# The last token tile of a hybrid decoder layer in halves, its routing with fewer dependent steps, one weight unit asked for sooner

## Chip, core and metric

One Trainium2 chip, one of its cores. The metric is the device time of one execution in microseconds, of the runs' median. The profile shows one more execution, taken by the hardware profiler.

## The reference, cut to what matters

One decoder layer over 512 prompt tokens and 8 sampled tokens (520 rows of 1024, float32). A mixer (a state-space part and a gated chunk part, joined by one output projection `w_out` and a residual add) is followed by a mixture of experts:

```
x = x + mix @ w_out
t = rmsnorm(x, norm2_g)
gl = t @ w_router_group + b;  gi = argmax(gl)              # 4 groups
el = (t @ w_router_expert + b)[group gi]                   # 8 experts in it
top 2 of softmax(el), weights normalised, times softmax(gl)[gi]
x = x + sum over the two experts e:  weight_e * (silu(t @ w_gate[e]) * (t @ w_up[e])) @ w_down[e]
y = rmsnorm(x, final_norm_g)
```

There are 32 experts with 1024x512, 1024x512 and 512x1024 weights each, 201 MB in all, every one of them read once.

## The kernel before

**Stages.** Everything is written out by hand in one program per engine, joined by semaphores. The first part (to about 190 us) is the mixer. Then come the five token tiles, in the order `ORDER = (0, 4, 1, 2, 3)`: 128 rows each, tile 4 the 8 sampled rows. `n` is the place in that order, `t` the tile, so `n = 4` is tile 3, the last. Each goes through the same steps:

- TensorE: output projection `out_half(t, j, halves)`, `j` the half of the mixer it takes, `halves` the 512-column halves of the result in `own[t]` (two PSUM banks). Tile 3's is spread between the other tiles' steps, and its last pieces are `out_half(3, 0, (0,))` and `out_half(3, 0, (1,))`. The semaphore `o_ps` counts finished tiles.
- VectorE: residual add into `x2` (loop at L1004, recorded as L694, the line of the helper `tt`; `o_ev`).
- ScalarE: `square` (L572, L574), `x2T_copy` (L587), `normed` (L579, with the store of the normalised rows to `hn2_d`, L581). VectorE: `root` (L955).
- TensorE: `turn` (eight transposes, L1363), `logits` (L1358, 36 columns).
- VectorE: `top_two` (L963 to L986): the best group, the two best experts as one-hot rows `oh12`, and their sum `ohb`. Of several equal values the first is taken, by a running count (`first_of`). The second expert's hits are found with the first one's taken out, so the two follow each other.
- TensorE: `count_before`, how many rows before this one go to the same expert. VectorE: `place` (L988 to L1002) makes of it the row's place `Wp` in the expert's list, the quotient `Wq` by 64 and remainder `Wr`; `row_oh` is the one-hot of the remainder over 64 places, `Wm` the mask of those with quotient 0, and `entry` the token number (two small parts, `vals`) of the masked rows at their expert's column.

**Table.** After the last tile ten small products (`row_oh` by `entry`, five tiles by two experts) give the table of 64 token numbers for each expert. `rows_of` (L1033) turns them into row numbers, an empty place into a large one (v = 0 gives 4000, out of bounds, so that the gather leaves it out). GpSimd then gathers the rows of experts 0 and 1 from `hn2_d` (`fetch_first`), and TensorE turns them (`x_T`). What does not fit an expert's 64 places goes through a second table (`xentry`, `further_table`) and loops of further steps.

**Experts.** 32 steps, each `gate_up`, a turn and `down` with 64 rows. The weights come as 96 units of 2 MB into a ring of ten places (`NSLOT = 10`), all issued by SyncE in order; `load(q)` is unit `q`:

```
            sp.wait_ge(wo_used, 1)
            load(6)
            store_x2(NT - 1)
            sp.wait_ge(o_ps, NT)
            sp.wait_ge(lg_ps, NT)
            load(7)
            sp.wait_ge(hn2_out[0], 48)
            sp.wait_ge(hn2_out[1], 32)
            load(8)
            sp.wait_ge(x2_out, 16 * NT)
            sp.wait_ge(xg_in[0], 16)
            load(9)
```

Places 6 to 9 hold other data in the first part, so these loads wait for it to be used: place 7 the half of `w_out` that the last `out_half` reads. Unit 10 and all behind it wait for the expert step that frees their place (`gu_half` halfway through `gate_up`, `gu_ps` at its end, `dn_ps` after `down`).

**Busy products.** `keep_busy(n)` is n products of the identity with itself, of two instructions each, whose result is not used. They fill TensorE's waits: 6 before the last count, 5 before the table, 12 and 8 between the table and the turn of the gathered rows.

Of the kernel before, what the change touches and what calls it, by code (L numbers as in the profile page):

```python
# [7 lines left out]
D = 1024  # L8
# [3 lines left out]
NT = 5  # L12
# [18 lines left out]
INVALID = 4000  # L31
# [9 lines left out]
def build(nc, a, o):  # L41
# [3 lines left out]
    with ctx:  # L45
# [107 lines left out]
        halfpi = tiny[:, 72:73]  # L153
        g2 = tiny[:, 84:92]
# [5 lines left out]
        def small(at, *shape):  # L160
            return view(23808 + at, *shape)
# [21 lines left out]
        sv = small(266, 2, 2)  # L183
# [143 lines left out]
        def _(sp):  # L327
# [96 lines left out]
        def _(act):  # L424
# [151 lines left out]
            def normed(n, t):  # L576
                r = ROWS[t]
                act.wait_ge(rt_rdy, n + 1)
# [104 lines left out]
        def _(dve):  # L683
# [255 lines left out]
            V.memset(Wq, 0.0)  # L939
            V.memset(Wm, 0.0)  # L940
# [22 lines left out]
            def top_two(n, t):  # L963
                r = ROWS[t]
                dve.wait_ge(lg_ps, n + 1)
                dve.wait_ge(rt_rdy, n + 1)
# [10 lines left out]
                mine, hit, count = (s32[0:r, k, :] for k in range(3))  # L977
# [4 lines left out]
                link(V.tensor_scalar(hit, mine, m8[0:r, t, 0:1], None, ALU.is_equal))  # L982
                link(first_of(oh1, hit, count))
                link(V.scalar_tensor_tensor(hit, mine, m8[0:r, t, 1:2], oh1, ALU.is_equal, ALU.is_gt))
                link(first_of(oh2, hit, count))
                tt(ohb[0:r, t, :], oh1, oh2, ALU.add).then_inc(oh_rdy, 1)  # L986

            def place(n, t):  # L988
# [5 lines left out]
                link(tt(s32[0:r, 3, 0:16].rearrange("p (j k) -> p j k", j=2), Wp[0:r, t, :].unsqueeze(2).to_broadcast([r, 2, 8]),  # L994
                        thr[0:r].unsqueeze(1).to_broadcast([r, 2, 8]), ALU.is_ge))
                link(V.tensor_reduce(Wq[0:r, t, :], s32[0:r, 3, 0:16].rearrange("p (j k) -> p j k", j=2), AX.X, ALU.add))
                V.scalar_tensor_tensor(Wr[0:r, t, :], Wq[0:r, t, :], float(-C), Wp[0:r, t, :], ALU.mult, ALU.add)
                link(V.tensor_scalar(Wm[0:r, t, :], Wq[0:r, t, :], 0.5, None, ALU.is_lt))
                tt(row_oh[0:r, t], rank_at[0:r].unsqueeze(1).to_broadcast([r, 2, C]), Wr[0:r, t, :].unsqueeze(2).to_broadcast([r, 2, C]), ALU.is_equal)
                link(tt(sv[0:r], vals[0:r, t], Wm[0:r, t, :].unsqueeze(2).to_broadcast([r, 2, 2]), ALU.mult))  # L1000
                tt(entry[0:r, t], oh12[0:r, t].unsqueeze(3).to_broadcast([r, 2, NE, 2]),
                   sv[0:r].unsqueeze(2).to_broadcast([r, 2, NE, 2]), ALU.mult).then_inc(slot_rdy, 1)  # L1002

            for n, t in enumerate(ORDER):  # L1004
# [12 lines left out]
                if n == 4:  # L1017
                    place(3, 2)
# [4 lines left out]
                if n == 3:  # L1023
# [4 lines left out]
                    place(2, 1)  # L1028
            top_two(4, 3)
# [3 lines left out]
            def rows_of(out, ps, n):  # L1033

                hi, lo = (ps[0:C, 0:2 * n].rearrange("c (t w) -> c t w", w=2)[:, :, w] for w in range(2))
                v, none, row, less = (ids[:, k, 0:n] for k in range(4))
                link(V.tensor_scalar(none, hi, 8.0, None, ALU.mult))
                link(tt(v, none, lo, ALU.add))
                link(V.tensor_scalar(none, v, 0.0, float(INVALID + 1), ALU.is_equal, ALU.mult))
                link(V.scalar_tensor_tensor(row, v, -1.0, none, ALU.add, ALU.add))  # L1040
                link(V.tensor_scalar(less, row, float(NTOK), float(-NTOK), ALU.is_ge, ALU.mult))
                tt(out[:, :, 0], less, row, ALU.add)
# [772 lines left out]
```

## Time and profile before

| | us |
|---|---|
| median of 3 runs | 762.81 (762.32 to 763.8) |
| profiled execution, as timed | 764.95 |
| its span in the profile | 763.2 |
| busy: TensorE products | 661.4 (87%) |
| busy: VectorE | 276.0 (36%) |
| busy: ScalarE | 160.6 (21%) |
| busy: GpSimd | 89.2 (12%) |
| weights and activations moved | 246.53 MB, mean 323 GB/s |

How to read it: times inside the profile count from the span's start. A line number is that of the kernel before. Many operations of VectorE go through one helper and carry its line, L694; all products carry L1358, all turns L1363, so they are told apart by their tiles and shapes. A float32 product appears as two MATMUL instructions. The DMA share is the mean busy share of the core's 16 DMA engines.

### The profile page before, as it was taken

The numbers are of one execution on the slowest core, as the hardware profiler recorded it, in microseconds if no ns is written. First come the engines' busy times: TensorE is split into PE (matmuls) and PEld (weight loads), VectorE is DVE, ScalarE is ACT, GpSimd is POOL, SyncE is SP. The second block draws the span as 40 slices with busy tenths as digits, with TensorE's granted clock in tenths as the row PEclk, the third lists the DMA queues.
The fourth block names the chain that finished last, engine by engine and source line by source line (L and its number), as shares of the span: only waits on it lengthen the run. The fifth ranks groups of instructions, "written<-read, shape, count | busy, mean of one in ns | idle before, by whom it ended". The sixth has DMA issues, their size and how long they took to land.

```text
span 763.2 us, 9485 instructions
## 1 busy us (share of the span) xinstructions
PE 661.4 (87%) x3284; PEld 322.6 (42%) x3284; DVE 276.0 (36%) x564; ACT 160.6 (21%) x314; POOL 89.2 (12%) x161
## 2 busy tenths in 40 slices
PE   8999989999997899996799997778777776769794
PEld 4488878854547433332233332223222222223231
DVE  7798994394475311210011121111111111112047
ACT  3687410321413011110111110101001110001023
POOL 4100000000001112121011211111111111111000
PEclk9999999999996899997899999999999999999998
DMA  9432017378247899999999999999999999999982
GB/s 331 191 110 112 1 40 280 135 314 381 88 165 284 307 406 403 396 390 388 427 416 398 411 408 394 418 406 410 413 395 401 405 413 406 402 398 415 421 329 112
DMA packets 29573, 246.53 MB, mean 323 GB/s; under 512 B 6578, under 2 KB 7090, under 8 KB 16592
## 3 DMA queue, kind: packets, MB, share of 16 engines
q1 hardware_dynamic: 22784, 233.95, 76.2%
q0 software_dynamic: 5280, 8.20, 3.3%
q10 hardware_dynamic: 1456, 3.62, 1.3%
q8 instruction: 41, 0.67, 0.4%
q14 instruction: 12, 0.10, 0.0%
HBM read 235.65 MB, written 19.20 MB: 334 GB/s over the span
## 4 chain that ended last, share of the span: by engine, by line
PE 51%; DMA 27%; DVE 13%; ACT 3%; another core or an unknown queue 3%; issue 2%; SPq 1%; ACTq 0%; POOLq 0%; DVEq 0%
PE psA L1358 27%; PE psB L1358 23%; DMA mem<-in_w_gu 19%; DMA mem<-in_w_down 5%; DVE mem L694 5%; DMA mem<-y_d 1%; DVE mem L918 1%; DVE mem L1173 1%; DMA mem<-in_w_vb 1%; DMA y_d<-mem 1%; ACT front_c L627 1%; PE psA L1363 1%; DVE mem L833 1%; PE psB L1363 1%
## 5 line engine op out<-in xcount | busy, mean ns | idle before, releaser
L1358 PE MATMUL psA<-mem 128*64 128x512 f32 (+8 forms) x1380 | 316.9, 521 | 39.9 <-DMA mem<-in_w_gu 20.6
L1358 PE MATMUL psB<-mem 128*64 128x512 f32 (+6 forms) x1242 | 276.0, 542 | 37.3 <-DMA mem<-in_w_gu 16.4
L1358 PEld LDWEIGHTS psA<-mem 128*64 128x64 f32 (+4 forms) x1380 | 148.4, 155 | 189.7 <-issue 139.2
L1358 PEld LDWEIGHTS psB<-mem 128*64 128x64 f32 (+2 forms) x1242 | 114.8, 155 | 180.0 <-issue 138.9
L694 DVE TENSOR_TENSOR mem<-mem 128x512 f32<-128x512 f32 (+21 forms) x124 | 68.1, 565 | 24.0 <-ACT mem L541 19.6
L1278 POOL DMA_INDIRECT y_d<-front_c,mem x30 | 27.5, 916 | 288.6 <-DVE front_c L1083 288.6
L1111 DVE TENSOR_TENSOR front_c<-front_c,psA 64x512 f32<-64x512 f32 x15 | 10.4, 690 | 122.5 <-ACT front_c L627 122.5
L1111 DVE TENSOR_TENSOR front_c<-front_c,psB 64x512 f32<-64x512 f32 x15 | 10.3, 690 | 122.1 <-ACT front_c L627 122.1
L1273 POOL DMA_INDIRECT mem<-hn_d,mem x34 | 33.3, 979 | 98.1 <-DVE mem L1043 70.5
L627 ACT ACTIVATE front_c<-psA 64x512 f32<-64x512 f32 x15 | 8.8, 588 | 125.8 <-PE psA L1358 125.8
L627 ACT ACTIVATE front_c<-psB 64x512 f32<-64x512 f32 x15 | 8.8, 588 | 116.5 <-PE psB L1358 116.5
L1083 DVE COPY front_c<-psA 64x512 f32<-64x512 f32 x15 | 10.4, 693 | 55.6 <-PE psA L1358 55.6
L1083 DVE COPY front_c<-psB 64x512 f32<-64x512 f32 x15 | 10.4, 693 | 52.6 <-PE psB L1358 52.6
L1363 PE MATMUL psA<-ident,mem 64*128 64x64 f32 (+2 forms) x200 | 19.1, 239 | 5.8 <-DMA mem<-hn_d,mem 4.5
L638 ACT ACTIVATE front_c<-psA 64x512 f32<-64x512 f32 x15 | 8.9, 591 | 71.0 <-PE psA L1358 71.0
L638 ACT ACTIVATE front_c<-psB 64x512 f32<-64x512 f32 x15 | 8.9, 590 | 69.9 <-PE psB L1358 69.9
L1363 PEld LDWEIGHTS psA<-ident,mem 64*128 64x128 f32 (+2 forms) x200 | 16.4, 142 | 9.7 <-issue 6.9
L1358 PE MATMUL psB<-ident 128*128 128x128 f32 x80 | 15.5, 376 | 3.4 <-POOL mem L1224 2.0
L694 DVE TENSOR_TENSOR mem<-psA,tiny 128x512 f32<-128x512 f32 x18 | 12.4, 691 | 10.4 <-PE psA L1363 8.6
L1363 PE MATMUL psB<-ident,mem 64*128 64x64 f32 (+1 forms) x152 | 13.5, 228 | 3.0 <-DVE mem L1098 3.0
L694 DVE TENSOR_TENSOR mem<-psB,mem 128x512 f32<-128x512 f32 (+2 forms) x23 | 15.0, 705 | 3.1 <-PE psB L1358 3.1
L1358 PEld LDWEIGHTS psB<-ident 128*128 128x128 f32 x80 | 14.6, 283 | 3.6 <-POOL mem L1224 2.0
(233 smaller groups left out, 373.7 us busy)
## 6 DMA issues: line engine op xcount, KB each, us to landing
mem<-in_w_gu SPq DMA_DIRECT2D x64, 2048.0 KB, 40.1
mem<-in_w_down SPq DMA_DIRECT2D x32, 2048.0 KB, 42.2
mem<-in_w_out SPq DMA_DIRECT2D x2, 2048.0 KB, 8.7
y_d<-mem SPq DMA_DIRECT2D x1, 4096.0 KB, 11.8
mem<-y_d SPq DMA_DIRECT2D x8, 512.0 KB, 9.1
mem<-in_x_T SPq DMA_DIRECT2D x8, 260.0 KB, 8.7
mem<-in_w_vb SPq DMA_DIRECT2D x8, 256.0 KB, 8.9
mem<-in_x_prompt SPq DMA_DIRECT2D x4, 512.0 KB, 11.1
```

The lines of the kernel that those rows point to most:

```text
L627: A(sg[64:128, u, :], ps[0:64, 1, :], ACT.Silu).then_inc(sg_rdy, 1)
L638: A(yst[0:C, u, 0:512], ps[0:64, 3, :], ACT.Copy).then_inc(y0_ev, 1)
L694: return V.tensor_tensor(out, x, y, op)
L833: V.tensor_copy(*u_copy(ql, e, 1))
L918: V.tensor_copy(mixA[32 * ql:32 * ql + 32, :, 0:NP_].rearrange("p m (b i) -> p i m b", i=T)[:, i], yg[32 * i:32 * i + 32, ql, :, NS:YC])
L1083: V.tensor_copy(yst[0:C, u, 512:1024], (psA, psB)[u][64:128, 3, :]).then_inc(y1_ev, 1)
L1111: V.tensor_tensor(hh[0:64, u, :], sg[64:128, u, :], ps[64:128, 1, :], ALU.mult).then_inc(h_done, 1)
L1173: ins = V.scalar_tensor_tensor(x2[0:r, t, :], yin[0:r, 2 * t + j, :], cw[0:r, j, t:t + 1], x2[0:r, t, :], ALU.mult, ALU.add)
L1273: return G.indirect_dma_start(out=dst, out_offset=None, in_=hn2_d[:, :], in_offset=bass.IndirectOffsetOnAxis(ap=rows_ap, axis=0), bounds_c ...
L1278: return G.indirect_dma_start(out=y2_d[:, :], out_offset=bass.IndirectOffsetOnAxis(ap=rows_ap, axis=0), in_=src, in_offset=None, bounds_ch ...
L1358: return nc.tensor.matmul(out, lhsT, rhs, start=start, stop=stop, skip_group_check=True)
L1363: return nc.tensor.transpose(out, in_, ident[b0:b0 + p, b0:b0 + p])
```

## The change

- Tile 3 is added (`add_half`), turned (`turn_half`), copied and multiplied with the router (`logits_half`) in two halves of 512 columns. `o_ps` now counts the two halves of its projection apart, the first at the end of `out_half(3, 0, (0,))`; the second to last places (`place(3, 2)`) stand between the two adds. The square is taken in halves too; the first half's mean enters the root as its bias.
- `top_two` finds both experts' hits from the values alone and counts both; where the two values are equal the second takes the second hit (`second` is 2 then, else 1). `entry` is made there, of the unmasked numbers.
- `place` compares the ranks with the place itself, without quotient, remainder or mask: a place of 64 or more matches none. Quotient, remainder and mask are made for all tiles together behind the first table, and `row_oh` once more with the remainder.
- The table products of the first four tiles go ahead of the last tile's count; two remain behind it. The busy products become 6, 2, 8 and 5 (from 6, 5, 12 and 8).
- `rows_of` needs no step for empty places: the token numbers are stored less 2048 (`EMPTY`), which is added back, so an empty place is 2048. The signal to GpSimd moves from the second output to the first; the second follows without one.
- SyncE issues unit 7 ahead of the last `x2` store and waits for the last projection only.

```diff
@@ SyncE
-                sp.wait_ge(o_ev, n + 1)
+                sp.wait_ge(o_ev, n + 1 if n < NT - 1 else NT + 1)
...
             load(6)
+            sp.wait_ge(o_ps, NT + 1)
+            load(7)
             store_x2(NT - 1)
-            sp.wait_ge(o_ps, NT)
             sp.wait_ge(lg_ps, NT)
-            load(7)
@@ ScalarE
-            for n in range(1, NT):
+            for n in range(1, NT - 1):
...
+            act.wait_ge(hn2_out[0], 32)
+            act.wait_ge(o_ev, NT)
+            A(hn2[:, 0, 0:512], x2[:, 3, 0:512], ACT.Square, accum_out=half_ss).then_inc(n2sq, 1)
+            for h in range(2):
+                act.wait_ge(x2T_ps, NT + h)
+                A(hn2T[:, 4 * h:4 * h + 4, :], own[3][:, h, :].rearrange("p (b n) -> p b n", n=128), ACT.Copy).then_inc(x2T_ev, 1)
+            act.wait_ge(o_ev, NT + 1)
+            A(hn2[:, 0, 512:1024], x2[:, 3, 512:1024], ACT.Square, accum_out=ss[:, 0, 3:4]).then_inc(n2sq, 1)
+            act.wait_ge(n2sq, NT + 1)
+            act.wait_ge(rt_rdy, NT)
+            A(ss[:, 1, 3:4], ss[:, 0, 3:4], ACT.Sqrt, scale=1.0 / D, bias=half_mean).then_inc(n2rt, 1)
+            normed(NT - 1, 3)
@@ VectorE, top_two
-                link(V.tensor_scalar(hit, mine, m8[0:r, t, 0:1], None, ALU.is_equal))
-                link(first_of(oh1, hit, count))
-                link(V.scalar_tensor_tensor(hit, mine, m8[0:r, t, 1:2], oh1, ALU.is_equal, ALU.is_gt))
-                link(first_of(oh2, hit, count))
+                V.tensor_scalar(hit1, mine, m1, None, ALU.is_equal)
+                V.tensor_scalar(hit2, mine, m2, None, ALU.is_equal)
+                link(V.tensor_scalar(second[0:r], m1, m2, 1.0, ALU.is_equal, ALU.add))
+                V.tensor_tensor_scan(count1, one32[0:r], hit1, 0.0, ALU.mult, ALU.add)
+                link(V.tensor_tensor_scan(count2, one32[0:r], hit2, 0.0, ALU.mult, ALU.add))
+                V.scalar_tensor_tensor(oh1, count1, 1.0, hit1, ALU.is_equal, ALU.mult)
+                link(V.scalar_tensor_tensor(oh2, count2, second[0:r], hit2, ALU.is_equal, ALU.mult))
                 tt(ohb[0:r, t, :], oh1, oh2, ALU.add).then_inc(oh_rdy, 1)
+                tt(entry[0:r, t], oh12[0:r, t].unsqueeze(3).to_broadcast([r, 2, NE, 2]),
+                   vals[0:r, t].unsqueeze(2).to_broadcast([r, 2, NE, 2]), ALU.mult)
@@ VectorE, last tile
+            dve.wait_ge(x_in[1], X_ROWS[1] * 16)
+            add_half(0)
+            place(3, 2)
+            dve.wait_ge(n2sq, NT)
+            V.tensor_scalar(half_mean, half_ss, 1.0 / D, EPS, ALU.mult, ALU.add).then_inc(rt_rdy, 1)
+            add_half(1)
+            root(4, 3)
             top_two(4, 3)
             place(4, 3)
@@ TensorE
-            out_half(3, 0, (0,))
+            out_half(3, 0, (0,)).then_inc(o_ps, 1)
...
             out_half(3, 0, (1,)).then_inc(o_ps, 1)
-            turn(4, 3)
-            logits(4, 3)
+            turn_half(0)
+            turn_half(1)
+            logits_half(0)
+            logits_half(1)
+            pe.wait_ge(slot_rdy, 4)
+            for n, t in enumerate(ORDER[0:4]):
+                table_rows(t, n == 0, False)
             keep_busy(6)
```

TensorE from the last output half (the first row) to the turn of the gathered rows (the last; `ident,mem 128x64`). Before:

```order
L1358 MATMUL psA<-mem 128x512 x4
L1363 MATMUL psA<-ident,mem 128x128 x8
L1358 MATMUL psA<-mem 128x36 x8
L1358 MATMUL psB<-ident 128x128 x6
L1358 MATMUL psA<-ohb,oneb 128x32 x4
L1358 MATMUL psA<-ohb,trib 128x32
L1358 MATMUL psB<-ohb,oneb 128x32 x5
L1358 MATMUL psB<-ident 128x128 x5
L1358 MATMUL psA<-mem 64x64 x10
L1358 MATMUL psB<-ident 128x128 x12
```

Changed:

```order
L1386 MATMUL psA<-mem 128x512 x4
L1391 MATMUL psA<-ident,mem 128x128 x8
L1386 MATMUL psA<-mem 128x36 x8
L1386 MATMUL psA<-mem 64x64 x8
L1386 MATMUL psB<-ident 128x128 x6
L1386 MATMUL psA<-ohb,oneb 128x32 x4
L1386 MATMUL psA<-ohb,trib 128x32
L1386 MATMUL psB<-ohb,oneb 128x32 x5
L1386 MATMUL psB<-ident 128x128 x2
L1386 MATMUL psA<-mem 64x64 x2
L1386 MATMUL psB<-ident 128x128 x8
```

Eight of the ten table products (64x64) have moved up behind the logits, ahead of the six busy products; seven busy products less stand on the way, counting those before the turn of the gathered rows (5, not 8; that turn and the register loads between stand behind the rows shown).

VectorE from the mask sum of the last tile (`ohb`) to the row numbers. Before:

```order
L694 TENSOR_TENSOR ohb<-mem 128x32
L694 TENSOR_TENSOR mem<-mem,psA 128x64
L993 TENSOR_REDUCE mem<-mem 128x2
L694 TENSOR_TENSOR mem<-mem 128x16
L996 TENSOR_REDUCE mem<-mem 128x2
L997 SCALAR_TENSOR_TENSOR mem<-mem 128x2
L998 TENSOR_SCALAR mem<-mem 128x2
L694 TENSOR_TENSOR mem<-mem 128x128
L694 TENSOR_TENSOR mem<-mem 128x4
L694 TENSOR_TENSOR mem<-mem 128x128
L1037 TENSOR_SCALAR mem<-psA 64x32
```

Changed:

```order
L707 TENSOR_TENSOR ohb<-mem 128x32
L707 TENSOR_TENSOR mem<-mem 128x128
L707 TENSOR_TENSOR mem<-mem,psA 128x64
L1011 TENSOR_REDUCE mem<-mem 128x2
L707 TENSOR_TENSOR mem<-mem 128x128
L1060 TENSOR_SCALAR mem<-psA 64x32
```

The entry (the first 128x128) now stands ahead of the row that waits for the count (`mem,psA`); behind that row two are left of eight.

SyncE's DMAs around the last x2 store:

```order
@@ -41,6 +41,6 @@
 L365 DMA x_d<-mem 128x1024 x2
 L329 DMA mem<-in_w_gu 128x4096
+L329 DMA mem<-in_w_down 128x4096
 L365 DMA x_d<-mem 128x1024
-L329 DMA mem<-in_w_down 128x4096
 L329 DMA mem<-in_w_gu 128x4096 x2
 L329 DMA mem<-in_w_down 128x4096
```

Unit 7 (`in_w_down`) is issued ahead of the last x2 store.

## Rows read from the trace of the kernel before

**Rows 1.** The page's second part: DMA's busy tenths in 40 slices of the span

```profile
DMA  9432017378247899999999999999999999999982
```

**Rows 2.** Stretches; busy us (count) of PE, PEld, DVE, ACT, POOL, clock, DMA share, GB/s

```profile
300.00:310.00 10.00, 9.80 (x54) 3.62 (x52) 1.38 (x2) 0.97 (x2) 2.26 (x4) 1.00 1.00 402
```

**Rows 3.** SyncE's timeline: start us, us, DMA issued, how many

```profile
229.36 0.32 SPq L365 DMA_DIRECT2D x_d<-mem  x1
235.58 0.33 SPq L329 DMA_DIRECT2D mem<-in_w_down  x1
236.32 13.24 SPq L329 DMA_DIRECT2D mem<-in_w_gu  x2
256.40 0.33 SPq L329 DMA_DIRECT2D mem<-in_w_down  x1
```

**Rows 4.** Stretches of 4 us around the first expert, columns as before

```profile
232.00:236.00 4.00, 4.00 (x19) 4.00 (x20) 0.41 (x2) 2.13 (x2) 0.00 (x0) 0.50 0.35 135
...
248.00:252.00 4.00, 4.00 (x41) 3.69 (x40) 0.47 (x1) 0.00 (x0) 0.00 (x0) 0.92 0.53 135
256.00:260.00 4.00, 4.00 (x22) 1.29 (x19) 0.62 (x4) 0.16 (x1) 0.52 (x1) 1.00 0.75 205
```

**Rows 5.** The chain that ended last, 225 to 262 us: start us, us, what

```profile
224.54 3.54 PE psA L1358 x8
228.10 1.24 DVE mem L694
...
229.42 1.16 ACT mem L572 x2
...
231.86 3.64 PE psA L1358 x16
...
235.53 0.27 DVE mem L968
...
238.86 0.21 DVE ohb L694
...
239.70 0.23 DVE mem L694
...
241.64 0.82 PE psA L1358 x10
242.49 0.20 DVE mem L1037
...
243.13 0.20 DVE mem L1040
...
243.88 6.97 PE psB L1358 x40
250.86 0.65 PE psA L1363 x8
...
252.70 7.11 PE psA L1358 x32
```

**Rows 6.** Groups by line and form: count, busy us, mean ns

```profile
L694 DVE TENSOR_TENSOR mem<-psB,tiny 128x512 f32<-128x512 f32 x1 | 0.7, 690 | 0.0
...
L562 ACT ACTIVATE front_c<-mem 128x520 f32<-128x520 f32 x4 | 2.5, 638 | 10.1 <-DVE mem L694 10.1
```

**Rows 7.** TensorE's timeline, three pieces: start us, us, what, count

```profile
218.59 1.87 PE L1358 MATMUL psB<-mem 128*128 128x36 f32 x16
...
229.39 1.09 PE L1363 MATMUL psA<-ident,mem 128*128 128x128 f32 x8 [1.32 <-DVE mem L694]
...
235.30 2.91 PE L1358 MATMUL psB<-ident 128*128 128x128 f32 x12
```

**Rows 8.** Us from issue to landing: gathers (L1273), weight units (L329); hn_d stores' median

```profile
DMA to landing us min/median/max: 3.1/8.8/9.2
...
DMA to landing us min/median/max: 7.7/8.6/11.1
...
hn_d<-mem ACTq DMA_DIRECT2D x4, 512.0 KB, 3.0
```

More of the change, by code:

```diff
@@ L30 @@
 EPS = 1e-6
-INVALID = 4000
+EMPTY = 2048
 TWO_PI = 2.0 * math.pi
@@ L153, in build @@
         halfpi = tiny[:, 72:73]
+        half_ss, half_mean, second = (tiny[:, 74 + k:75 + k] for k in range(3))
         g2 = tiny[:, 84:92]
@@ L976, in top_two @@
                 link(V.tensor_scalar(s4[0:r, 2, :], s4[0:r, 2, :], -1.0, BIG, ALU.add, ALU.mult))
-                mine, hit, count = (s32[0:r, k, :] for k in range(3))
+                mine, hit1, count1, hit2, count2 = (s32[0:r, k, :] for k in range(5))
                 link(tt(mine.rearrange("p (g e) -> p g e", g=NG), el.rearrange("p (g e) -> p g e", g=NG),
@@ L993, in place @@
                 link(V.tensor_reduce(Wp[0:r, t, :], pr[0:r], AX.X, ALU.add))
[L994 to L1004, printed above, removed]
+                tt(row_oh[0:r, t], rank_at[0:r].unsqueeze(1).to_broadcast([r, 2, C]),
+                   Wp[0:r, t, :].unsqueeze(2).to_broadcast([r, 2, C]), ALU.is_equal).then_inc(slot_rdy, 1)
+            for n, t in enumerate(ORDER[0:4]):
                 if t < 4:
@@ L1028, in _, with add_half @@
                     place(2, 1)
+            def add_half(h):
+                dve.wait_ge(o_ps, NT + h)
+                half = x2[:, 3, 512 * h:512 * h + 512]
+                tt(half, own[3][:, h, :], half, ALU.add).then_inc(o_ev, 1)
+            dve.wait_ge(x_in[1], X_ROWS[1] * 16)
[5 more added lines that the diff above has]
+            root(4, 3)
             top_two(4, 3)
@@ L1035, in rows_of @@
                 hi, lo = (ps[0:C, 0:2 * n].rearrange("c (t w) -> c t w", w=2)[:, :, w] for w in range(2))
[L1036 to L1040, printed above, removed]
+                high, row, less = (ids[:, k, 0:n] for k in range(3))
+                link(V.tensor_scalar(high, hi, 8.0, float(EMPTY), ALU.mult, ALU.add))
+                link(tt(row, high, lo, ALU.add))
                 link(V.tensor_scalar(less, row, float(NTOK), float(-NTOK), ALU.is_ge, ALU.mult))
-                tt(out[:, :, 0], less, row, ALU.add)
+                tt(out[:, :, 0], less, row, ALU.add).then_inc(tbl_rdy, 1)
                 return V.tensor_copy(out[:, :, 1], row)
             dve.wait_ge(tbl_ps, 1)
-            rows_of(tbl, psA[:, 3, :], NE).then_inc(tbl_rdy, 1)
+            rows_of(tbl, psA[:, 3, :], NE)
             R = lambda j: rs[:, j, :]
@@ L1513, in turn, with turn_half, logits_half, table_rows @@
                 ins.then_inc(x2T_ps, 1)
+            def turn_half(h):
+                pe.wait_ge(o_ev, NT + h)
+                for k in range(4):
+                    ins = tr(own[3][:, h, 128 * k:128 * k + 128], x2[:, 3, 512 * h + 128 * k:512 * h + 128 * k + 128])
+                ins.then_inc(x2T_ps, 1)
+            def logits_half(h):
+                pe.wait_ge(x2T_ev, NT + h)
+                for k in range(4 * h, 4 * h + 4):
+                    ins = mm(own[3][:, 0, 64 * 4:64 * 4 + 36], hn2T[:, k, :], wr[:, k, :], k == 0, k == KD - 1)
+                if h:
+                    ins.then_inc(lg_ps, 1)
+            def table_rows(t, first, last):
+                r = ROWS[t]
+                for j in range(2):
+                    ins = mm(psA[0:C, 3, 0:2 * NE], row_oh[0:r, t, j, :], entry[0:r, t, j].rearrange("p e w -> p (e w)"),
+                             first and j == 0, last and j == 1)
+                if last:
+                    ins.then_inc(tbl_ps, 1)
             def logits(n, t):
@@ L1577, in _ @@
             ins.then_inc(tot_ps, 1)
-            keep_busy(5)
+            keep_busy(2)
             pe.wait_ge(slot_rdy, NT)
-            for n, (t, j) in enumerate(itertools.product(range(NT), range(2))):
-                r = ROWS[t]
-                ins = mm(psA[0:C, 3, 0:2 * NE], row_oh[0:r, t, j, :], entry[0:r, t, j].rearrange("p e w -> p (e w)"), n == 0, n == 2 * NT - 1)
-            ins.then_inc(tbl_ps, 1)
+            table_rows(3, False, True)
             pe.wait_ge(tbl_rdy, 1)
```

26 lines of the change are left out of this document (15 added, 11 removed).

## The prediction

> **What bounds the kernel now.** Read first the DMA line of the 40 slices [rows 1]: from the slice that begins at 267 us to the last but one, every digit is 9 or nearly so, while the slices before it are half empty. The stretches say it more sharply: at 300 us the 16 DMA engines are busy for the whole of their time at 402 GB/s [rows 2], but 0.53 of 248 to 252 us and 0.75 of 256 to 260 us [rows 4]. So there are two programs. Up to about 257 us a chain of small dependent steps sets the pace, and behind it the weight stream does.
>
> Who starts the stream? SyncE's own timeline [rows 3] shows weight unit 7 (the w_down row) at 235.58, unit 8 at 236.32, and unit 9 as the second of that pair, 13.24 us further down, so at 249.2: it waits for the first gather of rows. Unit 10 goes out at 256.40, halfway through the first expert. The ring has ten places, so all 86 units from 10 to 95 wait for an expert to be done with an old one. 86 units of 2048 KB are 180 MB; at 402 GB/s that is 449 us, from 257 to 706, and the queue never runs dry in between. Each microsecond that unit 10 goes out sooner is a microsecond off the end; a DMA made faster or sooner before it is worth nothing.
>
> So the question is how soon the first expert begins, and the chain of waits answers it [rows 5]: the last output half ends at 228.08, the residual add takes 1.24 us, then come square, copy and turn, the logits from 231.86, the choice of experts from 235.53 to 238.86, the places from 239.70, the table product at 241.64, the row numbers from 242.49, **6.97 us of products that only keep TensorE busy** from 243.88, the turn of the gathered rows (it begins with that piece's end, about 250.8), the first expert at 252.70.
>
> **The change, step by step** (all against the profiled execution: span 763.2 us, 764.95 us as timed).
>
> *Last tile in halves.* Before, nothing of tile 3 starts until 228.08, then 7.45 us pass to 235.53. After, the first half (added on VectorE while the second output half still runs, since the first output half is complete before 224.54) is only to be turned. From 228.08: add of the second half 0.69 [rows 6] to 228.8, meanwhile the first four turns; the other four (eight took 1.09 [rows 7]) to 229.35; on ScalarE the copy of half two, 0.6 by the 0.64 of a 520-column piece [rows 6], to 229.95. Then two branches. ScalarE: square of a half and the reading of its sum, 0.8 (whole they took 1.16 [rows 5], and a 520-column piece alone is 0.64 [rows 6]), then root and reciprocal of one column, some 0.5: 231.3. TensorE: the logits' first half runs beside that copy, so the 1.87 us of a whole logits product [rows 7] end near 231.2. The choice starts at 231.3, not 235.53: **4.2 us**. The bound below: before, the granted clock was 0.50 (the lower level, 1.2 GHz) in 232 to 236 us [rows 4] and this product took 3.64 us [rows 5], after three microseconds in which TensorE had only the turns to do. If it is at that level in the new order too, the logits end near 233.0, so 2.5 us. The new order leaves TensorE hardly a gap from 224.5 to 231, so I take 4.2.
>
> *Both experts side by side.* From the first hit to the mask sum there were seven dependent steps of some 0.25; now the two hits, the two counts and the two results follow each other without a wait between, and one small comparison is added. Such a step begins 0.21 after the one it depends on (three between 242.49 and 243.13 [rows 5]); one that depends on nothing begins sooner, I assume half of that. I count **0.3 us** (0.1 to 0.5). The entry product moves ahead of the place, behind the mask sum, where VectorE waits for TensorE anyhow (238.86 plus 0.2 to 239.70).
>
> *Places without a mask.* From 239.70 to 241.64, 1.94 us, nine instructions. Now three: product, sum and the wide comparison, twice 0.25 and 0.3, some 0.8. **1.1 us** (0.9 to 1.3). The quotient and remainder come later, for all tiles at once, behind the row numbers: five instructions, the last with 640 columns of output (512 took 0.69 [rows 6]), some 1.7 us, before the second table. That is only asked for behind the turn of the gathered rows, and VectorE has the whole wait for the gather, 243.88 to 250.8, for it: hidden, and if the cover should be short, at most a microsecond.
>
> *Table products.* Ten took 0.85, from 241.64 to 242.49; eight go ahead of the six busy products, where TensorE waits for the choice; two remain, 0.35. **0.5 us.** Their cover: logits end 231.3, eight products 0.7, twelve busy instructions 1.5 (full clock) to 2.9 (as at 235.30 [rows 7]), so TensorE is free between 233.5 and 234.9, and is asked for the mask sum at 234.5. It may be 0.3 late; I take that off.
>
> *Row numbers.* Two dependent steps of 0.21 [rows 5] go, and the signal moves ahead of the last copy (0.1): **0.5 us**.
>
> Sum to the first row table: 4.2 + 0.3 + 1.1 + 0.5 + 0.5 - 0.3 = 6.3, so 243.84 becomes 237.5.
>
> *Behind the table.* Twenty busy products (40 instructions) took 6.97 us and were longer than the gather, which was home at 249.2 (unit 9 went out on it [rows 3]), 5.4 us behind the table. Thirteen remain: 4.5 us at the same mix, 6.3 if each takes the 0.24 us of the twelve at 235.30 [rows 7]. The gather can now be the longer one: 5.4 if as before. It may be more, since unit 8 is then still in flight: gathers of 240 to 300 us land 3.1 to 9.2 us after their issue, median 8.8 [rows 8], and 3.1 was this one, since its issue took 1.0 and began 0.9 behind the table. I take 6.2 us for the later of the two: **0.7 us** (from +1.5 to -3.7).
>
> *Eighth unit sooner.* It goes out at about 228.3 instead of 235.58, into an idle DMA, but unit 9 and unit 10 wait for experts and not for it. Worth nothing by itself. It passes the last x2 store on SyncE's queue; that store is only asked for by unit 9. What it may cost is the normalised rows' store, issued at 232.6 instead of 232.9 and 3.0 us long when alone [rows 8]. It is home near 236, when the table is not (237.5), if it is not stretched by more than 1.5 us. Here the Trainium skill speaks against the change (DMA: Bandwidth & Descriptors, section Queues, rings and completion order): an engine takes turns between queue rows packet by packet, and a completion write goes out only after every earlier write of that engine, whatever its queue. By that the gather would be home no sooner than unit 8, and this part would be worth about nothing instead of 0.7. The trace agrees in kind: gathers beside the full queue take 8.8 us, not 3.1 [rows 8]. As a mechanism of its own it is rival B.
>
> Sum: 6.3 + 0.7 = **7.0 us** until the first expert, 245.7 instead of 252.70; unit 10 near 249.4. Against the profiled execution that is 764.95 - 7.0 = 757.95; the median of the runs shown, 762.81, stands 2.1 below it, and the prediction is given against the median: 762.81 - 7.0 = **755.8 us**.
>
> **The rivals.**
> *A, the clock in the first expert.* If the busy products run at full clock they end before the gather, TensorE idles some three microseconds, and the first expert begins at half clock, as the logits ran at 232. Half clock over 5 us of it loses 2.5. For it: busy products cut from 20 to 13, a longer wait; after the gaps at 228 to 232 the clock read 0.50 [rows 4]. Against: the busy products of before began at half clock (40 in 6.97, against 0.24 each at half), and 248 to 252 us reads 0.92 [rows 4]: full when the expert came. 7.0 - 2.5 = 4.5, so 758.3.
> *B, the gather behind unit 8.* Landing takes 8.8 and not 3.1: the turn comes 10.9 us after the table, 3.9 later than before, so 6.3 - 3.9 = 2.4 is left: 760.4.
> *C, slower: store and gather both behind weight units.* The store of the normalised rows, issued at 232.6, takes the 9.2 us of the slowest gather and not 3.0 [rows 8], home at 241.8; SP and GpSimd wait for it (unit 8 and the gather). Then 0.9 to the gather, 1.0 to issue, 8.8 to land: 252.5, against 250.8 before. Loss 1.7, so 764.5. It decides where the two landings together pass 16.3 us (they were 6.1). Against: unit 7 has over 4 us of head start, and units issued here are home after 7.7 at the least [rows 8], 5.2 of them at 402 GB/s, so little of it is left when the store is issued.
> *D, no effect:* the stream is not what ends last, or the shifted start meets another floor: 762.8. Against it speaks that no stretch behind 257 us has idle DMA.
> *E, more:* the gather as quick as before and the clock full: 6.6 + 1.5 = 8.1, so 754.7.
>
> **How the numbers follow.** Forecast 0.52; A 0.22; B 0.10; C 0.03; D 0.03; E 0.10. The range takes the forecast, A and E with their unknowns, and B's near part: 753.8 to 760.2. A measurement of this kernel tells 0.2%, 1.5 us, from nothing. Faster by more than that: all but C, D and a slice of B, 0.92; same 0.05; slower 0.03.
>
> **What would show it.** In the chain of waits of after: choice of experts for the last tile some 3 us behind the last output half and not 7.45; three instructions between the last places' wait and the table; the table 6.3 us sooner; the first expert at about 245.7. In the DMA timeline unit 7 at 228, unit 8 unmoved, units 9 and 10 sooner by what the first expert is. From there to the end the same distances as before. Wrong it would be if the first expert starts 7 us sooner and the end does not follow, or if SyncE's unit 8 goes out later than 237.

## The result and the profile after

| | before | changed |
|---|---|---|
| median of 8 runs each | 763.56 (762.32 to 764.78) | 766.31 (765.04 to 767.32) |
| ratio | | 1.0027, 95% interval 1.0014 to 1.0040 |
| span of the profiled execution | 763.2 | 765.6 |

The changed kernel is slower, by 0.27% or about 2.1 us by the ratio; the two medians lie 2.75 us apart. The forecast was 7 us the other way, and the result lies outside the range.

The chain of waits of the changed kernel from the last output half to the second expert (start us, us, what) tells it in nine rows:

```profile
228.47 0.70 DVE mem L707
...
230.40 0.72 ACT mem L610 x2
...
231.67 1.16 ACT mem L579
...
232.84 8.31 DMA hn_d<-mem
...
242.10 8.32 DMA mem<-hn_d,mem
...
250.47 1.11 PE psA L1391 x8
...
252.79 9.65 PE psA L1386 x32
...
262.47 0.60 ACT front_c L640
...
265.01 8.67 PE psB L1386 x32
```

Against [rows 5]: the add, the half square and the copy of the normalised rows end at 232.82. Then two DMAs stand in the chain where products and VectorE steps stood, 8.31 us for the store of the last normalised rows, and 8.32 us for the first gather. The turn of the gathered rows begins at 250.47 and not at 250.86, the first expert at 252.79 against 252.70. And that expert takes 9.65 us, not 7.11.

Where was the routing? VectorE's timeline (start, us, line, operation, names and shapes) shows it done long before. The rows are the logits' scaling, the mask sum, the first step of the last tile's places and the first of the row numbers:

```profile
231.75 0.26 DVE L980 SCALAR_TENSOR_TENSOR mem<-psA,tiny,mem 128x36 f32<-128x36 f32 x1
...
234.86 0.19 DVE L707 TENSOR_TENSOR ohb<-mem 128x32 bf16<-128x32 f32 x1
...
235.63 0.22 DVE L707 TENSOR_TENSOR mem<-mem,psA 128x64 f32<-128x64 f32 x1 [0.37 <-PE psA L1386]
...
236.77 0.18 DVE L1060 TENSOR_SCALAR mem<-psA 64x32 f32<-64x32 f32 x1 [0.34 <-PE psA L1386]
...
237.52 0.17 DVE L1064 CAST mem<-mem 64x32 int32<-64x32 f32 x1
```

Choice at 231.75, mask sum at 234.86, places from 235.63, row numbers from 236.77, table ready at 237.6. Before it was ready at 243.84 [rows 5]. But GpSimd issues the gather only when the store is home as well, and that was 3.5 us later, at 241.15. What was worked out for these engines came, and nothing of it reached the first expert.

SyncE's timeline answers to [rows 3]:

```profile
228.46 0.33 SPq L329 DMA_DIRECT2D mem<-in_w_down  x1
229.19 0.33 SPq L365 DMA_DIRECT2D x_d<-mem  x1
241.22 9.60 SPq L329 DMA_DIRECT2D mem<-in_w_gu  x2
259.03 0.33 SPq L329 DMA_DIRECT2D mem<-in_w_down  x1
```

Unit 7 goes out 7.1 us sooner; unit 8, which waits for the same store as the gather, goes out at 241.22 instead of 236.32; unit 10 at 259.03 instead of 256.40. The stretches answer to [rows 4] and [rows 2] (columns as there); the first row is the kernel before, the others are the changed one:

```profile
228.00:300.00 72.00, 63.64 (x361) 33.62 (x362) 25.19 (x96) 11.66 (x19) 9.12 (x15) 0.88 0.87 340
...
228.00:300.00 72.00, 58.69 (x329) 28.10 (x329) 22.41 (x83) 10.92 (x19) 9.10 (x15) 0.88 0.86 327
232.00:236.00 4.00, 2.65 (x28) 2.31 (x29) 3.21 (x19) 2.10 (x2) 0.00 (x0) 1.00 1.03 322
248.00:252.00 4.00, 1.53 (x16) 1.41 (x16) 0.38 (x1) 0.00 (x0) 0.00 (x0) 0.50 0.34 79
256.00:260.00 4.00, 4.00 (x16) 1.17 (x14) 0.50 (x4) 0.00 (x0) 0.37 (x1) 0.76 0.49 180
```

The clock is at full level in 232 to 236 us, where it was at half before, and at half in 248 to 252, just ahead of the first expert, where it was 0.92. The DMA share is 0.34 and 0.49 in the last two stretches (0.53 and 0.75 before). Over 228 to 300 us the DMAs moved 327 GB/s, before 340. That is 13 GB/s over 72 us, 0.94 MB, or 2.3 us at 402 GB/s, and the span grew by 2.4.

### The profile page after: what moved, and what is told of

Same layout as the page of the kernel before. It is cut to its first block, busy times and chain, and to the rows that moved or that the text cites. A ratio compares the mean times of both kernels' runs of the same rounds, so it can differ in the third digit from the quotient of the medians.

```text
span 765.6 us, 9429 instructions
## 1 busy us (share of the span) xinstructions
PE 659.7 (86%) x3264; PEld 317.9 (42%) x3264; DVE 272.9 (36%) x546; ACT 161.1 (21%) x317; POOL 89.2 (12%) x161
## 4 chain that ended last, share of the span: by engine, by line
PE 55%; DMA 28%; DVE 10%; ACT 3%; another core or an unknown queue 2%; issue 2%; SPq 0%; POOLq 0%; DVEq 0%
PE psA L1386 28%; PE psB L1386 25%; DMA mem<-in_w_gu 13%; DMA mem<-in_w_down 11%; DVE mem L707 4%; DVE mem L931 1%; DMA mem<-in_w_vb 1%; DMA mem<-hn_d,mem 1%; DMA hn_d<-mem 1%; ACT front_c L640 1%; PE psB L1391 1%; PE psA L1391 1%; DVE mem L846 1%; ACT mem L648 1%
## 5 line engine op out<-in xcount | busy, mean ns | idle before, releaser
L707 DVE TENSOR_TENSOR mem<-mem 128x512 f32<-128x512 f32 (+17 forms) x116 | 67.7, 598 | 23.7 <-ACT mem L541 19.6
L1391 PEld LDWEIGHTS psB<-ident,mem 64*128 64x128 f32 (+1 forms) x152 | 11.7, 139 | 6.6 <-issue 6.6
L1386 PE MATMUL psB<-ident 128*128 128x128 f32 x60 | 10.9, 355 | 2.9 <-POOL mem L1252 2.0
```

What stands on the lines that cost most here:

```text
L707: return V.tensor_tensor(out, x, y, op)
L1386: return nc.tensor.matmul(out, lhsT, rhs, start=start, stop=stop, skip_group_check=True)
L1391: return nc.tensor.transpose(out, in_, ident[b0:b0 + p, b0:b0 + p])
```

## The experiments

Twelve kernels in three groups, each timed beside the kernel before. A DMA is called home when it has landed, so when the engines that wait for it may go on. Half clock is a granted clock of 0.50, the lower level. Two suspects stood first: transfers that stand behind weight units, and the clock in the first expert. A third question came out of the first group: what the end of the kernel really follows.

### Unit 7 behind the store

```diff
-            sp.wait_ge(o_ps, NT + 1)
-            load(7)
             store_x2(NT - 1)
+            sp.wait_ge(o_ps, NT + 1)
             sp.wait_ge(lg_ps, NT)
             sp.wait_ge(hn2_out[0], 48)
             sp.wait_ge(hn2_out[1], 32)
+            load(7)
             load(8)
```

(Against the changed kernel, as every edit below unless it says otherwise.)

> The changed kernel with one difference: weight unit 7 is issued only once the last store of the normalised rows is home, together with unit 8. Theory (the store stands behind unit 7): the store takes 3 to 3.5 us instead of 8.3, the first gather is issued at about 238.5 instead of 242.1, but now has two units (10 us of transfer) ahead of it and lands near 249; first expert near 251.3, time 1.5 to 3 us below the changed kernel, near before (763 to 765). Rival (the clock in the first expert alone made the loss): the time stays at the changed kernel's. Rival (gathers are quick beside one or two units): gather home by 244, time near 758.

Ratio to before 1.0004 (0.9987 to 1.0022), median 763.81. The store's landing line, and the gather and the first expert in the chain of waits:

```profile
DMA to landing us min/median/max: 2.6/2.7/3.1
```

```profile
238.56 9.47 DMA mem<-hn_d,mem
...
248.07 1.11 PE psA L1391 x8
...
250.39 9.04 PE psA L1386 x32
```

The store takes 2.6 to 3.1 us. The gather goes out at 238.56, takes 9.47 with two units ahead of it, and the first expert begins at 250.39, at half clock (9.04 us long). Near what was expected; the loss is gone, nothing is won.

### The last x2 store behind the store

```diff
             load(7)
-            store_x2(NT - 1)
             sp.wait_ge(lg_ps, NT)
             sp.wait_ge(hn2_out[0], 48)
             sp.wait_ge(hn2_out[1], 32)
+            store_x2(NT - 1)
             load(8)
```

> The changed kernel with the last x2 store moved behind the store of the normalised rows on SyncE's side; unit 7 stays sooner. If the store of the normalised rows stands behind all that is queued ahead of it: home 1.3 us sooner (about 239.8), everything behind follows, time about 1 us below the changed kernel. If it was the x2 store alone that held it up: home near 236.5, the gather issued at 238.5, time 3 to 5 us below. If neither: 8.3 us and no difference.

Ratio 1.0023 (1.0007 to 1.0039), median 765.34. The slowest store is now 5.7 us, issued at 232.36 and home at 238.0: 2.6 us shorter, twice what was expected, so the x2 store had held it up too. But the gather, with unit 8 and the x2 store just ahead, took 9.72 instead of 8.32 and gave 1.4 us of it back; the first expert began at 251.06, again at half clock (8.65 us).

### Busy products until the gather is home

```diff
-            keep_busy(5)
+            keep_busy(38)
             pe.wait_ge(xg_in[0], 16)
```

> The changed kernel with 38 instead of 5 busy products ahead of the turn of the gathered rows, so that TensorE has work almost until the gather is home (250.4). Theory (half the clock in the first expert costs 2.5 us, and every microsecond of the first expert's end is one of the whole): the first expert takes 7.1 us instead of 9.65, time 2 to 3 us below the changed kernel, equal to before within 1 us. Rival (the weight stream, with its idle time before unit 10, sets the end by itself): first expert quick, but the time as the changed kernel's.

Ratio 0.9994 (0.9976 to 1.0011), median 763.45. The chain of waits:

```profile
237.39 13.49 PE psB L1386 x92
250.88 0.65 PE psA L1391 x8
...
252.60 7.11 PE psA L1386 x32
```

TensorE is busy for 13.49 us, the first expert begins at 252.60, as in the changed kernel, and takes 7.11 us. With that alone the loss is gone. Store and gather are nearly as slow as without this edit (7.5 us, and 8.4 from the start of the gather's issue to unit 9, which goes out on it); they have eaten the gain, and the clock made the loss.

### Only the sooner unit, in the kernel before

This edit is made to the kernel before:

```diff
-            store_x2(NT - 1)
             sp.wait_ge(o_ps, NT)
-            sp.wait_ge(lg_ps, NT)
             load(7)
+            store_x2(NT - 1)
+            sp.wait_ge(lg_ps, NT)
```

> The kernel before with only the eighth unit sooner. Theory: the store of the normalised rows takes 8 us instead of 3.3 (home near 241), unit 8 follows it 5 us later than before, and the first gather, issued as before at 244.7, has as much of the unit ahead of it as before had of units 7 and 8; so the time is that of before, within 1.5 us, and nothing is won by the sooner unit. Rival (a weight unit sooner is 5 us of transfer won): 2 to 5 us faster than before.

Ratio 1.0030 (1.0012 to 1.0048), median 766.3: slower, where I had expected no difference. The store took 8.1 us and unit 8 went out at 241.19, both as expected; the first expert began at 253.35 instead of 252.70. Its profiled span, 763.9, is only 0.7 above that of before. The rest is a matter of which execution was profiled: that of before, timed at 764.95, lies 1.1 us above the median of the runs beside this kernel (763.85), that of this kernel (765.81) 0.5 below its own. So the trace of this kernel can show 0.9 of the 2.4 us and no more. That part of the change is worth nothing or less by itself.

### Unit 7 right behind the store, with 5 and with 17 busy products

```diff
+            store_x2(NT - 1)
             sp.wait_ge(o_ps, NT + 1)
+            sp.wait_ge(hn2_rdy, NT)
             load(7)
-            store_x2(NT - 1)
```

and for the second `keep_busy(17)` in the place of `keep_busy(5)`.

> The changed kernel with unit 7 issued when the last normalised rows are ready, so right behind their store and not 4.4 us ahead of it. If what is ahead in the engines' queues holds the store up: the store takes 3 to 4 us (home by 236.5), unit 8 goes out at 236.5, the gather has unit 7's tail and unit 8 ahead of it and lands near 245.5 to 246.5 (248 when both went out at 236), first expert near 248, perhaps at half clock: 760 to 763. If the store suffers from any unit beside it, whatever the order: 6 to 8 us long, time 764 to 766.

> The same with 17 instead of 5 busy products ahead of the turn, to keep the clock until the gather is home. If the clock in the first expert adds its own part: first expert 7.1 us, 1 to 2.5 us below u7_with_store, 759 to 761. If not: the same as u7_with_store.

Ratios 1.0026 (1.0013 to 1.0040) and 1.0019 (1.0008 to 1.0030), where 760 to 763 had been the theory: a miss, though the time of the second alternative. The unit goes out 0.06 us behind the store and the store is nearly as slow as in the changed kernel:

```profile
232.39 7.88 DMA hn_d<-mem
...
241.21 8.37 DMA mem<-hn_d,mem
...
249.62 1.12 PE psA L1392 x8
```

```profile
232.45 0.33 SPq L329 DMA_DIRECT2D mem<-in_w_down  x1
240.32 9.65 SPq L329 DMA_DIRECT2D mem<-in_w_gu  x2
```

So it isn't only what is ahead in the queues: a unit issued with the store holds it up by 5 us (7.88 against 2.6 to 3.1). The queues (packets, MB, share of the 16 engines' time) show how. q10 carries ScalarE's DMAs, here the store, q1 those of SyncE. First the changed kernel, 232.84 to 236.50 and 236.50 to 241.50:

```profile
q1 hardware_dynamic: 97, 0.97, 92.4%
...
q10 hardware_dynamic: 144, 0.52, 25.6%
q1 hardware_dynamic: 116, 0.42, 20.4%
```

Then this kernel, 232.40 to 236.00 and 236.00 to 240.50:

```profile
q1 hardware_dynamic: 32, 0.52, 55.4%
q10 hardware_dynamic: 57, 0.23, 17.7%
...
q1 hardware_dynamic: 108, 1.57, 81.6%
q10 hardware_dynamic: 87, 0.29, 15.9%
```

In the changed kernel not one packet of the store moved in the 3.7 us behind its issue, while unit 7 and the x2 store did; all 144 came behind 236.5. Here the store's packets moved beside the unit's from the start, and the last of them all the same only when the unit was nearly through: the store was home at 240.27, the unit (8.4 us from its issue) at 240.85. So a small DMA was late in two ways, behind the unit or shared out along it.

Near this place (behind the logits, about a microsecond ahead of the store) the kernel before would have put unit 7, once the logits come as early as they do now; just that order was not run. With the unit beside the store the routing part of the change loses even without the sooner unit; with the unit held until the store is home, as in the first experiment, it doesn't. Twelve more busy products kept TensorE until 246.4, 4.2 us short of the turn at 250.50; the clock fell all the same and the first expert took 9.07. So that kernel didn't test what it was for.

### What the end follows: units held behind the gather

Unit 8 held (the edit of unit 7 right behind the store, and in addition the one shown), then both held, with `load(7)` moved behind that same wait:

```diff
             sp.wait_ge(hn2_out[1], 32)
+            sp.wait_ge(xg_in[0], 16)
             load(8)
```

> Unit 7 right behind the store, unit 8 held until the first gather is home. Theory: gather with at most unit 7's tail ahead of it, 5.5 to 6.5 us, home at 244 to 245, first expert at 246.5; but DMA idles from 239 to 245, and units 8 and 9 then stand ahead of unit 10, whose transfer begins near 255.5 instead of 257 to 258: 761 to 763. Rival (the first expert's start sets the end): 757.5.

> Units 7 and 8 both held until the first gather is home, so nothing is beside the store and the gather: store 3 us, gather 5.4 us, first expert at 245.7 to 246, as the prediction had it. Theory (the end is the weight stream's start plus its bytes, and units 7 to 9 are part of the stream as soon as it never rests behind them): 89 units from about 244.5 are 86 from 260, so 2 to 3 us slower than before, though the first expert begins 7 us sooner. Rival (the prediction's own view: each microsecond that the first expert begins sooner is one off the end): 756 to 757.

Ratios 0.9993 (0.9981 to 1.0005) and **1.0016 (1.0003 to 1.0029)**. With unit 8 held, the store took 7.96 us beside unit 7, the gather alone 3.22, and the first expert began at 246.52; the clock fell as it began and it took 8.81. With both held, nothing is beside the store and the gather. TensorE's timeline, and SyncE's:

```profile
241.86 0.70 PE L1393 MATMUL psA<-ident,mem 64*128 64x64 f32 x8
...
244.15 7.09 PE L1388 MATMUL psA<-mem 128*64 128x512 f32 x32 [0.43 <-DVE mem L709]
```

```profile
241.90 0.33 SPq L329 DMA_DIRECT2D mem<-in_w_down  x1
242.28 0.90 SPq L329 DMA_DIRECT2D mem<-in_w_gu  x2
247.84 0.33 SPq L329 DMA_DIRECT2D mem<-in_w_down  x1
```

```profile
228.00:300.00 72.00, 66.63 (x395) 31.02 (x395) 24.38 (x86) 12.50 (x22) 11.92 (x19) 0.98 0.85 334
```

The gather is home at 241.9, the first expert begins at 244.15 at full clock, **8.5 us sooner than before**, unit 10 goes out at 247.84 instead of 256.40. And the kernel is slower than before. The view of the prediction, that each microsecond of unit 10 is one off the end, falls with this run. Units 7, 8 and 9 now begin at 242 and the stream never rests behind them: three units more to move, 15.6 us at 5.2 each, from 15 us sooner. Over 228 to 300 us it moved 334 GB/s, less than before's 340.

### The gather alone, and unit 7 where it does not hurt

Three kernels made from this: unit 7 as in the change, the last x2 store behind the store, unit 8 behind the gather; the same with unit 7 in two halves; and the changed kernel with unit 8 behind the gather and nothing else.

```diff
             load(7)
-            store_x2(NT - 1)
             sp.wait_ge(lg_ps, NT)
             sp.wait_ge(hn2_out[0], 48)
             sp.wait_ge(hn2_out[1], 32)
+            store_x2(NT - 1)
+            sp.wait_ge(xg_in[0], 16)
             load(8)
```

> The changed kernel with unit 7 where it is (228.5), the last x2 store behind the store of the normalised rows, and unit 8 behind the first gather. Theory (a store or a gather beside a weight unit takes 5 to 6 us more than alone, and the end is the bytes moved by the time the stream never rests): store home at 238, gather issued at 239 and home at 242.3 (3.3 us), first expert at 244.5 at full clock, unit 8 from 243: one unit more moved by 300 us than with both units behind the gather (334 GB/s over 228 to 300 us, so 349 to 360 here), time 760 to 762, faster than before. Rival (only the total idle of the first expert's wait counts, not what is moved in it): as both_behind_gather.

Ratio **0.9972 (0.9960 to 0.9984)**, median 761.97.

```profile
232.33 6.04 DMA hn_d<-mem
...
239.32 3.47 DMA mem<-hn_d,mem
...
244.75 7.11 PE psA L1387 x32
```

```profile
228.00:300.00 72.00, 65.46 (x384) 30.66 (x384) 24.38 (x86) 12.49 (x22) 11.40 (x19) 0.95 0.91 359
244.00:248.00 4.00, 3.31 (x18) 1.20 (x18) 3.42 (x20) 0.00 (x0) 0.97 (x2) 1.00 0.84 332
```

The gather takes 3.47 us and the first expert begins at 244.75 at full clock, about as with both units held; but unit 7 is already home, and 359 GB/s were moved, not 334. That is 1.8 MB more, most of one unit, or 4.5 us at 402 GB/s; the two ratios lie 0.0044 apart, 3.4 us.

With unit 7 in halves (the diff is against gather alone), the first where unit 7 stood, the second behind the store (`PRIOR` of place 7 is then 4, for its one more signal):

```diff
+            def half_7(h):
+
+                e, j = UNITS[7]
+                src = w_dn[e] if j == 2 else w_gu[2 * e + j]
+                cols = slice(2048 * h, 2048 * h + 2048)
+                sp.dma_start(ring[:, 7, cols], src[:, cols]).then_inc(w_full[7], 16)
...
-            load(7)
+            half_7(0)
...
             store_x2(NT - 1)
+            half_7(1)
             sp.wait_ge(xg_in[0], 16)
```

> The same with unit 7 as two DMAs of half the columns: the first at 228.5 (home near 234), the second when the store is home. The store then has half as much ahead of it: home near 235.5 to 236.5, ahead of the table (237.6); the second half stands beside the gather: 2.6 us of transfer more ahead of it, home at 243.5 to 245. Theory: within 1.5 us of gather_alone, either way. If descriptors and not bytes hold the gather up, it lands at 247 as beside a whole unit: 762 to 764.

Ratio **0.9956 (0.9939 to 0.9972)**, median 761.4, the lowest of all, though its interval meets that of gather alone. The store is home at 235.8, and the gather waits for the table again and not for it (issued at 238.43, home by 243.1, the second half unit beside it). The first expert begins at 245.0.

> The changed kernel with one wait more: unit 8 behind the first gather. Store as in the changed kernel (home 241.2), gather alone 3.3 us instead of 8.3 (home 245.4), first expert at 247.5 and, TensorE having waited less, mostly at full clock; unit 8 from 246.3. Theory: 345 to 350 GB/s over 228 to 300 us, time 763 to 764, 2 to 3 us below the changed kernel.

Ratio 0.9986 (0.9974 to 0.9999), median 762.96: one more wait on SyncE turns the changed kernel's loss into a small gain. The gather took 3.19 us, the first expert began at 246.32, but at half clock, 10.05 us long.

The last one makes the edit of the x2 store, with the sooner unit 7, to the kernel before, whose table comes at 243.8. Unit 8 isn't held in it, so its partner is "the last x2 store behind the store" (1.0023) and not gather alone:

> The kernel before with unit 7 sooner and the last x2 store behind the store of the normalised rows: store home near 238.5, unit 8 from 239.5 to 245, all of it home before the first gather (issued 244.7 as before) has much to wait: gather 3.5 to 5 us. The 20 busy products hold TensorE until 250.8 all the same, so first expert as before. Theory: time as before, within 1 us (340 to 343 GB/s over 228 to 300 us).

Ratio 0.9995 (0.9978 to 1.0011), median 763.89: no difference. The order of the DMAs is needed for the gain, since the changed kernel loses without it. Whether the shorter routing chain is needed too was not tested: the kernel before with unit 8 held behind the gather was not run.

### All runs by one measure

For each profiled execution the bytes moved over 228 to 300 us, what the difference to before's 340 GB/s makes at 402 GB/s (72 us times the difference, by 402), and how its span stands to before's 763.2 ("half" where the granted clock was at or fell to 0.50 as the first expert began):

| kernel | first expert at | GB/s | us by the bytes | span difference | ratio of the runs |
|---|---|---|---|---|---|
| changed | 252.79, half clock | 327 | +2.3 | +2.4 | 1.0027 |
| unit 7 behind store | 250.39, half | 348 | -1.4 | -1.2 | 1.0004 |
| x2 behind store | 251.06, half | 344 | -0.7 | +0.2 | 1.0023 |
| busy until gather | 252.60 | 345 | -0.9 | -2.1 | 0.9994 |
| before, unit 7 sooner | 253.35 | 338 | +0.4 | +0.7 | 1.0030 |
| unit 7 with store | 251.94, half | 334 | +1.1 | -0.7 | 1.0026 |
| the same, more busy | 252.82, half | 332 | +1.4 | +0.7 | 1.0019 |
| unit 8 behind gather too | 246.52, half | 349 | -1.6 | -1.7 | 0.9993 |
| both behind gather | 244.15 | 334 | +1.1 | +1.4 | 1.0016 |
| gather alone | 244.75 | 359 | -3.4 | -2.9 | 0.9972 |
| the same, halves | 245.00 | 356 | -2.9 | -2.5 | 0.9956 |
| unit 8 behind gather | 246.32, half | 350 | -1.8 | -2.4 | 0.9986 |
| before, x2 behind | 251.89 | 349 | -1.6 | -2.0 | 0.9995 |

The start of the first expert does not give the time: the kernel that starts it first, at 244.15, is slower than before, and the one with 252.60 isn't. The bytes moved by 300 us give each execution's span to about a microsecond (1.8 for unit 7 with the store). One profiled execution is not the median of its kernel: the single executions of one kernel differ by 1.4 to 5 us. That of before, timed at 764.95, lies 0.6 to 1.4 us above the medians of before in the four rounds (763.56 to 764.4), so the span differences read about a microsecond lower than the ratios.

## Why the prediction was wrong

**The chain to the table: right.** 6.3 us were predicted, 243.84 to 237.5; it came at 237.6, and the output half had ended 0.4 later. By terms: halves 3.8 (said 4.2), both experts 0.2 (0.3), places 1.1 (1.1), table products 0.6 (0.5), row numbers 0.5 (0.5); the 0.3 taken off for a late TensorE did not come. The clock stayed full behind the halves, as assumed. VectorE's work for the second table stayed hidden, but for 0.56 us that a product waited for it with both units held.

**"It is home near 236, when the table is not (237.5)": this is the step that failed first.** The store took 8.31 us. I had taken 3.0 from its rows alone, all of them made beside an idle or nearly idle DMA, and argued that unit 7 would be almost home. With its 4.4 us of head start the unit alone held the store for 3 us (5.7 to 6.0 in three kernels), the x2 store between them for the rest. From the table to the turn, where the sum had 6.2 us, it took 12.9: 3.5 until the store was home, 0.9 to the gather's issue, 8.3 for the gather. The rule of the Trainium skill that I had weighed here (DMA: Bandwidth & Descriptors, section Queues, rings and completion order: turns between queues packet by packet, and a completion write only after every earlier write of that engine) named the right danger; I applied it to the gather alone, where it was to cost 0.7 us. The trace agrees with what it was to do there in two kernels, where the gather was home 0.2 us behind unit 8 (249.4 and 249.2 with busy until the gather, 249.6 and 249.4 with unit 7 right behind the store), and not in the one with unit 7 behind the store, where it was home at 248.03 and unit 8 at 249.9. Of the turns, the queues show them for the store with the unit issued beside it, and none for 3.7 us in the changed kernel. Rival C, store and gather both behind units, stood at 3 in 100. By its measure, two landings together past 16.3 us, they were 8.31 and, from the end of the issue, about 7.2 (8.32 less the 1.16 of issuing in GpSimd's timeline); it fell short of the point by a microsecond, so this part alone ended level with before (250.47 against 250.86).

**"I take 6.2 us for the later of the two": the second.** The gather took 8.3 us beside unit 8, and takes 3.2 to 3.5 alone (three kernels), from the same rows whose 3.1 to 9.2 us I had as bounds. The 3.1 was also misread: it is the second gather's, issued at 246.20; the first, issued at 244.74, took 4.4 us to 249.2, with the units issued at 235.58 and 236.32 nearly through. Mine had a whole one in flight. (B's 10.9 us is 10.7 by its own terms, 0.9, 1.0 and 8.8; nothing hangs on it.)

**The clock in the first expert (rival A) came on top.** It was put at 2.5 us, and cost 9.65 less 7.11. I held the two rivals apart, as alternatives; they are one event, since a late gather is what leaves TensorE idle. The thirteen busy products behind the table (of before's twenty; three more were taken out ahead of it, ten in all) ended at 242.3, 8.1 us before the gather. C's 764.5 and A's 2.5 make 767.0, near the 766.31 measured.

**"Each microsecond that unit 10 goes out sooner is a microsecond off the end; a DMA made faster or sooner before it is worth nothing": the third, and the deepest.** It holds only while the DMAs rest somewhere behind unit 9. What counts is the time the DMA engines rest before the stream never rests again, wherever that lies: units 7 to 9 are part of the stream. It made me price the sooner unit at nothing, though gather alone, which had it home early, moved 1.8 MB more than the kernel that held it, and gained where that one lost; and it would have given 756 for a kernel that took 765.6. (The stream's end, put at 706 us from 86 units at 402 GB/s, left out the tokens' own reads and writes: the last unit goes out at 679.77, and the engines stay full at 407 GB/s until 740.) Even with 8.5 us on the first expert, no kernel here gained more than 3.4 us.

**Both criteria came.** SyncE's unit 8 went out later than 237, which was named as what would show the prediction wrong; so was a first expert 7 us sooner whose end doesn't follow, and that is the kernel with both units held.

**Still open:** why the store's packets wait for a unit that is 4.4 us ahead and move beside one issued with it; why the cost of the fallen clock doesn't follow the idle time; and what makes the kernel before with the sooner unit 2.4 us slower, of which its bytes show 0.4.

## What to carry to other kernels

When a chain is shortened, look at what ran beside it and was hidden by it. Here the store of the normalised rows had 11 us before the table was ready (232.88 to 243.84), where even 8 us of it would not have shown; in the changed kernel it had 4.8. And the prediction took its length from rows without asking what ran beside them. Where a bandwidth-bound stream follows a latency-bound start, count the time in which the DMAs rest and not the time at which the first consumer begins, and let small transfers that something waits for go alone, with the large ones before or behind them. How long a transfer takes depends on what else is in flight, here 2.6 us or 8.3 for the same store; a row taken beside idle queues is a lower bound.

## What was not expected of the hardware

- A gather of 64 rows, from the start of its issue to the turn behind it: 3.2 to 3.5 us alone, 4.7 beside half a unit, 8.3 to 9.7 beside one or two weight units of 2 MB that went out ahead of it, though such a unit is itself only 5.2 us of transfer.
- A store of 512 KB: 2.6 to 3.1 us alone, 3.2 with half a unit 4.4 us ahead, 5.7 to 6.0 with a whole one, 7.5 to 8.3 with a unit and another 512 KB store ahead, 7.9 to 8.0 with a unit issued with it.
- The store's packets: none moved in the 3.7 us behind its issue with unit 7 4.4 us ahead; 57 of 144 in the first 3.6 us with the unit issued 0.06 us behind it. Either way the store took about 8 us (8.31 with an x2 store ahead as well, and 7.88).
- TensorE's idle time just ahead of the turn of the gathered rows, and the length of the first expert behind it: 8.1 us idle and 9.65 us (the changed kernel), 6.8 and 8.65 (x2 behind the store), 6.5 and 9.53 (unit 7 with the store), 5.8 and 9.04 (unit 7 behind the store), 4.2 and 9.07 (the 17 busy products), 3.1 and 10.05, 2.8 and 8.81 (the two with unit 8 behind the gather and the turn near 244). With 0.9 us idle or less it took 7.11 in each of the four kernels that had it (busy until the gather, gather alone, the same with halves, both behind the gather). So the cost didn't grow with the idle time: it was 1.5 to 2.9 us in all seven kernels that paid it.
